# Prompt differential attention as eight one-turn stages over 43 turns, with two pairs of score banks and a late reciprocal

## The reference

```
x = x + 1/2 * SwiGLU_1(RMSNorm(x))
h = RMSNorm(x); P = h @ w_in
   group A: gated DeltaNet, 4 heads of 128, blocks, a state carried from block to block
   group B: differential attention, 4 heads, two softmax maps per head (64 wide each), values 128 wide
            s_m = q_m k_m^T / 8, prompt: block-causal mask of 64 frames; streams: all 512 cached keys + 16 new ones
            out = (softmax(s_0) - lam * softmax(s_1)) V, then RMSNorm per head and head gain
x = x + concat(A, B) @ w_out
x = x + 1/2 * SwiGLU_2(RMSNorm(x))
```

## Time and profile before

| what | us |
|---|---|
| median of 3 runs | 1477.61 |
| lowest, highest | 1477.19, 1478.74 |
| the profiled execution, its own time | 1481.6 |
| its span, first to last instruction | 1479.8 |
| PE busy | 1383.9 (94%) |
| DVE busy | 922.7 (62%) |
| ACT busy | 667.2 (45%) |
| POOL busy | 352.4 (24%) |
| mean granted clock of PE, share of full speed | 0.973 |

### The profile page before, as it was taken

One profiled execution on the slowest core, in us unless ns is written; L12 is line 12 of the kernel. 1 busy time (PEld: TensorE's weight loads), 2 busy tenths in 40 slices (PEclk: granted clock), 3 DMA queues, 4 the chain that ended last, 5 costly groups with the idle time before them and its releaser, 6 DMA issues.

```text
span 1479.8 us, 24346 instructions
## 1 busy us (share of the span) xinstructions
PE 1383.9 (94%) x8677; PEld 1249.3 (84%) x8677; DVE 922.7 (62%) x1485; ACT 667.2 (45%) x1255; POOL 352.4 (24%) x240
## 2 busy tenths in 40 slices
PE   5999999999997999999987878779999999999999
PEld 5999999988886998787876765458999999998887
DVE  4876666644446676648546765754687777764444
ACT  6555555533334553533344332443555555543333
POOL 0645555500000000212121321000354444420000
PEclk9999999999998999999998899899999999999999
DMA  6222222270101422111022025490122222235000
GB/s 188 68 85 85 85 85 85 85 298 0 29 0 35 137 71 90 44 43 58 1 79 80 0 75 182 168 315 16 58 73 85 85 86 86 85 113 211 16 20 35
DMA packets 139254, 127.27 MB, mean 86 GB/s; under 512 B 3781, under 2 KB 107845, under 8 KB 139196
## 3 DMA queue, kind: packets, MB, share of 16 engines
q1 hardware_dynamic: 136684, 117.15, 24.7%
q0 software_dynamic: 2512, 9.34, 1.8%
HBM read 115.83 MB, written 10.39 MB: 85 GB/s over the span
## 4 chain that ended last, share of the span: by engine, by line
PE 82%; DVE 11%; ACT 3%; issue 2%; DMA 1%; POOL 0%; SPq 0%; DVEq 0%; ACTq 0%
PE psum_all L918 22%; PE psum_all L920 22%; PE psum_all L919 22%; PE psum_all L928 6%; PE psum_all L1782 2%; DVE hw_lo L329 1%; PE psum_all L1795 1%; PE psum_all L1898 1%; PE psum_all L492 1%; ACT pr L2113 1%; PE psum_all L1787 1%; DMA K_c<-cache_k 0%; DMA x_tok<-x_prompt 0%; PE psum_all L2159 0%; DVE hT_lo L479 0%
## 5 line engine op out<-in xcount | busy, mean ns | idle before, releaser
L918 PE MATMUL psum_all<-hw_hi,gu_op 128*128 128x320 f32 x1200 | 373.0, 311 | 9.4 <-DVE gu_op L559 4.7
L920 PE MATMUL psum_all<-hw_hi,gu_op 128*128 128x320 f32 x1200 | 373.4, 311 | 0.0
L919 PE MATMUL psum_all<-hw_lo,gu_op 128*128 128x320 f32 x1200 | 371.9, 310 | 0.0
L918 PEld LDWEIGHTS psum_all<-hw_hi,gu_op 128*128 128x128 f32 x1200 | 227.4, 189 | 10.2 <-issue 5.2
L919 PEld LDWEIGHTS psum_all<-hw_lo,gu_op 128*128 128x128 f32 x1200 | 229.2, 191 | 0.0
L920 PEld LDWEIGHTS psum_all<-hw_hi,gu_op 128*128 128x128 f32 x1200 | 226.7, 189 | 0.0
L574 DVE TENSOR_TENSOR gu_op<-w_sum,gu_op 128x512 fp32r<-128x512 f32 x160 | 173.0, 1082 | 55.2 <-ACT gu_op L570 51.3
L799 POOL TENSOR_TENSOR w_sum<-raw_gu 128x512 f32<-128x512 f32 x80 | 129.6, 1620 | 223.2 <-DVE gu_op L574 222.6
L918 PE MATMUL psum_all<-wd_hi,a_hi 128*128 128x512 f32 x440 | 171.4, 390 | 1.7 <-DVE x_tok L936 1.7
L595 DVE TENSOR_TENSOR a_lo<-aT,a_hi 128x640 fp32r<-128x640 f32 x88 | 72.6, 825 | 160.6 <-ACT a_hi L587 160.6
L920 PE MATMUL psum_all<-wd_hi,a_lo 128*128 128x512 f32 x440 | 171.3, 389 | 0.0
(11 more groups left out here) (359 smaller groups left out, 2473.4 us busy)
## 6 DMA issues: line engine op xcount, KB each, us to landing
raw_gu<-ffn_w_gu SPq DMA_DIRECT2D x80, 512.0 KB, 4.6
wd<-ffn_w_down SPq DMA_DIRECT2D x2, 4096.0 KB, 20.8
raw_b<-w_in SPq DMA_DIRECT2D x8, 1024.0 KB, 5.2
K_c<-cache_k SPq DMA_DIRECT2D x8, 1024.0 KB, 8.4
V_c<-cache_v SPq DMA_DIRECT2D x8, 1024.0 KB, 5.3
wd<-ffn_w_down SPq DMA_DIRECT2D x2, 3584.0 KB, 12.0
raw_cv<-w_in SPq DMA_DIRECT2D x13, 512.0 KB, 4.0
wd<-ffn_w_down SPq DMA_DIRECT2D x6, 1024.0 KB, 4.9
```

The lines of the kernel that those rows point to most:

```text
L918: nc.tensor.matmul(out, lhs_hi, rhs_hi, start=start, stop=False, skip_group_check=True)
L919: nc.tensor.matmul(out, lhs_hi, rhs_lo, start=False, stop=False, skip_group_check=True)
L920: return nc.tensor.matmul(out, lhs_lo, rhs_hi, start=False, stop=stop, skip_group_check=True)
```

## The change

The prompt attention becomes eight stages of one turn each: scores, maximum, exps (probs), combine, transposes (TURN), their copy (TURNED), values, output copy (OUT). Unit u starts at turn 2u for u under 12 and at 26, 29, 32, 35 for the last four; stage s of unit u is in turn START[u] + s. `att_turns` has START[15] + 7 + 1 = 43 turns. Scores of even units go to banks 0 and 1, those of odd ones to 2 and 3. The transposes go to bank 4; the values of units 0 to 11 to the last quarter of bank 4, those of the last four units to a score bank that is free by then. Within a turn PE does transposes, values, scores; DVE combine, maximum; ACT the copy of the transposes, the output copy, the exps. The combination becomes e1 * (-lam * sum0 / sum1) + e0, without the pass over the second map (L2085 goes, and L2083 becomes a scalar_tensor_tensor of one element), and the first map's reciprocal, kept for four units in `inv_sum`, is a scale in ACT's copy of the output.

```diff
+        inv_sum = late.put("inv_sum", [P, 4, MAPS])
...
+        START = [2 * u if u < 12 else 26 + 3 * (u - 12) for u in range(len(UNITS))]
+        AT_TURN = {at: u for u, at in enumerate(START)}
+        (SCORES, MAXIMUM, PROBS, COMBINE, TURN, TURNED, VALUES, OUT) = range(8)
+
+        def att_turns(stages):
+
+            for turn in range(START[-1] + OUT + 1):
+                for stage, do in stages:
+                    if turn - stage in AT_TURN:
+                        do(AT_TURN[turn - stage])
+                yield
+
+        def values_out(u):
+
+            if UNITS[u][0] < 3:
+                return psum[4][:, 3 * P:4 * P]
+            return psum[2 * ((u + 1) % 2)][:, 0:P]
...
-                if u:
-                    pe.wait_ge(N["probs"], 2 * u)
+                if u >= 2:
+                    pe.wait_ge(N["probs"], 2 * (u - 1))
+                if u >= 15:
+                    pe.wait_ge(N["pv_copied"], u - 2)
...
+                    bank = psum[2 * (u % 2) + m]
...
+                if u >= 2:
+                    pe.wait_ge(N["pv_copied"], min(u, 12) - (u < 12))
                 for k in range(qt + 1):
-                    last = nc.tensor.transpose(psum[2][:, hc(k)], pc[:, hc(k)], ident)
+                    last = nc.tensor.transpose(psum[4][:, hc(k)], pc[:, hc(k)], ident)
...
+                if qt == 3:
+                    pe.wait_ge(N["probs"], 2 * min(u + 2, len(UNITS)))
+                elif u:
                     pe.wait_ge(N["pv_copied"], u)
...
+            yield from att_turns(((TURN, transposes), (VALUES, values), (SCORES, scores)))
...
-                link(dve, "att_chain", c + 2, V.reciprocal(soft[:, 6:8], soft[:, 4:6]))
-                link(dve, "att_chain", c + 3, V.tensor_tensor(soft[:, 8:9], soft[:, 7:8],
-                                                              lam[:, 7:8], ALU.mult))
-                link(dve, "att_chain", c + 4, V.tensor_scalar(pr[:, 1, 0:n], pr[:, 1, 0:n],
-                                                              soft[:, 8:9], None, ALU.mult))
+                if u >= 4:
+                    dve.wait_ge(N["pv_copied"], u - 3)
+                link(dve, "att_chain", COMBINE_LINK[u], V.reciprocal(inv, soft[:, 4:6]))
+                link(dve, "att_chain", COMBINE_LINK[u] + 1, V.scalar_tensor_tensor(
+                    soft[:, 8:9], soft[:, 4:5], inv[:, 1:2], lam[:, 7:8], ALU.mult, ALU.mult))
                 if u:
                     dve.wait_ge(N["p_tr"], u)
-                V.scalar_tensor_tensor(pc[:, 0:n], pr[:, 0, 0:n], soft[:, 6:7], pr[:, 1, 0:n],
+                V.scalar_tensor_tensor(pc[:, 0:n], pr[:, 1, 0:n], soft[:, 8:9], pr[:, 0, 0:n],
                                        ALU.mult, ALU.add).then_inc(N["pcomb"], 1)
-                dve.wait_ge(N["pcomb"], u + 1)
...
+            yield from att_turns(((COMBINE, combine), (MAXIMUM, maximum)))
...
+                act.wait_ge(N["nmax"], u + 1)
+                if u:
+                    act.wait_ge(N["pcomb"], u)
+                for m in range(MAPS):
+                    nc.scalar.activation(pr[:, m, 0:n], psum[2 * (u % 2) + m][:, 0:n], ACT.Exp,
...
+                act.wait_ge(N["pv_mm"], u + 1)
+                if u < 11:
+                    act.wait_ge(N["p_tr"], u + 2)
+                nc.scalar.activation(q_tok[:, qt, hc(h)], values_out(u), ACT.Copy,
+                                     scale=inv_sum[:, u % 4, 0:1]).then_inc(N["pv_copied"], 1)
+
+            yield from att_turns(((TURNED, turned), (OUT, out), (PROBS, probs)))
...
-            c = 4 * len(UNITS)
+            c = 3 * len(UNITS)
```

More of the change, by code:

```diff
@@ L2028, in scores @@
                 n = P * (qt + 1)
-                if u:
-                    pe.wait_ge(N["probs"], 2 * u)
+                if u >= 2:
+                    pe.wait_ge(N["probs"], 2 * (u - 1))
+                if u >= 15:
+                    pe.wait_ge(N["pv_copied"], u - 2)
                 for m in range(MAPS):
                     rows = slice(DK * m, DK * m + DK)
-                    nc.tensor.matmul(psum[m][:, 0:n], qT[rows, h, qt * P:(qt + 1) * P],
+                    bank = psum[2 * (u % 2) + m]
+                    nc.tensor.matmul(bank[:, 0:n], qT[rows, h, qt * P:(qt + 1) * P],
                                      kTn[rows, h, 0:n], start=True, stop=False,
                                      skip_group_check=True)
-                    last = nc.tensor.matmul(psum[m][:, n - 64:n], late_neg[rows, :],
+                    last = nc.tensor.matmul(bank[:, n - 64:n], late_neg[rows, :],
                                             late_one[rows, :], start=False, stop=True,
@@ L2060, in att_pe @@
             pe.wait_ge(N["qkT_copied"], 13)
-            for u in range(len(UNITS) + 1):
-                if u < len(UNITS):
-                    scores(u)
-                if u:
[L2065 to L2077, removed]
+            yield from att_turns(((TURN, transposes), (VALUES, values), (SCORES, scores)))
@@ L2078, in att_dve, with maximum, combine @@
+        def att_dve(dve):
+            def maximum(u):
+                n = P * (UNITS[u][0] + 1)
+                dve.wait_ge(N["sc_mm"], u + 1)
+                if u:
+                    dve.wait_ge(N["probs"], 2 * u)
+                s = 2 * (u % 2)
+                link(dve, "att_chain", MAX_LINK[u],
+                     V.tensor_reduce(soft[:, 0:2], psum_all[:, s:s + 2, 0:n], AX.X, ALU.max))
                 V.tensor_scalar(soft[:, 2:4], soft[:, 0:2], -(DK ** -0.5), None, ALU.mult)\
                     .then_inc(N["nmax"], 1)
-                yield
+            def combine(u):
+                n = P * (UNITS[u][0] + 1)
+                inv = inv_sum[:, u % 4, :]
@@ L2090, in att_dve @@
                                        ALU.mult, ALU.add).then_inc(N["pcomb"], 1)
-                dve.wait_ge(N["pcomb"], u + 1)
-                yield
-            yield
-            yield
-        def att_act(act):
[L2097 to L2116, removed]
@@ new lines, in att_dve, with links @@
+            yield from att_turns(((COMBINE, combine), (MAXIMUM, maximum)))
+        def links():
+            n, of_max, of_combine = 1, {}, {}
+            for turn in range(START[-1] + OUT + 1):
+                if turn - COMBINE in AT_TURN:
+                    of_combine[AT_TURN[turn - COMBINE]] = n
+                    n += 2
+                if turn - MAXIMUM in AT_TURN:
+                    of_max[AT_TURN[turn - MAXIMUM]] = n
+                    n += 1
+            return of_max, of_combine
@@ L2117, in att_act, with turned, probs, out @@
+        MAX_LINK, COMBINE_LINK = links()
+        def att_act(act):
+            def turned(u):
+                n = P * (UNITS[u][0] + 1)
+                act.wait_ge(N["p_tr"], u + 1)
                 if u:
                     act.wait_ge(N["pv_mm"], u)
-                    nc.scalar.activation(q_tok[:, qt, hc(h)], psum[3][:, 0:P], ACT.Copy)\
-                        .then_inc(N["pv_copied"], 1)
-                yield
+                nc.scalar.activation(pT[:, 0:n], psum[4][:, 0:n], ACT.Copy)\
+                    .then_inc(N["p_copied"], 1)
+            def probs(u):
+                n = P * (UNITS[u][0] + 1)
+                act.wait_ge(N["nmax"], u + 1)
[3 more added lines that the diff above has]
+                    nc.scalar.activation(pr[:, m, 0:n], psum[2 * (u % 2) + m][:, 0:n], ACT.Exp,
+                                         bias=soft[:, 2 + m:3 + m], scale=DK ** -0.5,
+                                         accum_out=soft[:, 4 + m:5 + m])\
+                        .then_inc(N["probs"], 1)
+            def out(u):
+                qt, h = UNITS[u]
+                act.wait_ge(N["pv_mm"], u + 1)
[4 more added lines that the diff above has]
+            yield from att_turns(((TURNED, turned), (OUT, out), (PROBS, probs)))
```

3 lines of the change are left out of this document (1 added, 2 removed).

## The result

The changed kernel takes 1495.2 us (median of 4 runs, 1494.7 to 1500.2); the kernel before, measured beside it, 1478.2 us. The ratio is 1.012, 95% interval 1.0094 to 1.0146: **17 us slower**. Forecast was 9.6 us slower, 1487.2, with a range of 1477 to 1497: the measured time lies in the range, near its upper end.

The account below looks back on a forecast made before the run. Latency, not a full engine, was taken to bound the kernel. The terms 893.5 + 34.3 + 24.40 + 21.05 + 15.3 gave 988.6 against 978.95, so 9.6 us slower: 1487.2 us, range 1477 to 1497.

Parts of the forecast that it names:

- The nine turns that att_turns adds: End of the cache attention: 25 lone turns instead of 16, costing 15.3 us, bounds 14.8 and 17.5.
- rival D: Tail of the cache attention: the nine turns cost nothing, only the 4.7 us gain shows, 1472.9 us; chance 0.04.
- rival A: Turns 8 to 42: attention hides, pairs near 4.51 us, 9.9 us faster, 1467.7 us; chance 0.08.
- likeliest case: Whole kernel: the prediction's own sum, 1487.2 us, with its own range of 1482 to 1493; chance 0.62.
- rival C: Turns 8 to 42: PE's clock at 0.74 in place of 0.88, 6 us more, 1493 us; chance 0.17.
- L2085's removal: DVE's combine at 384 columns: 0.46 us less, 1.05 us instead of 1.51.
- so 4.7 us are won: Turns 8 to 42: turn 42 ends at 893.5 instead of 898.2, a gain of 4.7 us.
- Quiet pair: Two turns in tile 3 with 384 keys: 5.37 us against 5.26 before, so nothing won.
- The pair beside POOL's z products: Tile 3: 7.56 us loses L2085's 1.39, about 0.4 comes back as waiting; the next pair saves 0.9.
- Hold at tile 4: DVE beside POOL's three products: the combine escapes, Xm is held but ends 4.7 us ahead, between 3 and 6.7.
- Added turns before tile 4's first product: Tile 4's start: maximum, exps, values and scores stand in front; the lead falls from 4.9 to 2.8 us.
- Rule against trace: DVE and POOL at tile 4: by the skill's port lock Xm is held for one product, not three, 2 us more gained.

Follow-up runs that it names:

- e2: The kernel before with only the late reciprocal (new combination and scale in the output copy), stages and 34 turns as they were: 1472.6 us, ratio 0.9961.
- e3: The changed kernel with the old combination (pass over the second map, no scale in the output copy): 1503.3 us, ratio 1.015.
- e11: The changed kernel measured and traced a second time, nothing altered: 1496.1 us, ratio 1.012.
- e8: The changed kernel with its stages in 39 turns (last four units earlier, two pairs of stages sharing a turn): 1490.0 us, ratio 1.0089.
- e5: The changed kernel with POOL's three products for tile 4 waiting for DVE's five scaling operations: 1494.3 us, ratio 1.0105.
- e7: The kernel before with the late reciprocal, K_c loaded ahead of V_c, and POOL's tile 4 products behind DVE's scaling operations: 1472.9 us, ratio 0.9953.
- e10: The changed kernel in 39 turns, with K_c loaded ahead of V_c and POOL's tile 4 products behind DVE's scaling operations: 1489.0 us, ratio 1.0066.
- e1: The kernel before with nine empty turns between the prompt attention and the cache attention: 1501.5 us, ratio 1.0141.

## Why the prediction was right, and by how much it was off

**Direction and cause: right.** The nine turns that att_turns adds are what is paid. Forecast 15.3 us for them. Behind tile 4's last product, where the forecast as a whole had +13 (15.3, less 1 in the streams and 1.4 right behind the product), the six traces with 43 turns and the old order of loads show +13.5 to +16.1, the two with the turns empty (+15.2, +15.7) among them. That this could be hidden (rival D) and that attention hides in the delta chain (rival A) both fall.

**The size: forecast 9.6 us, measured 17.** 1495.2 us is also outside the likeliest case's own range, which ended at 1493; the stated range reached to 1497 for the sake of rival C. That the time fell inside it is in part luck.

**L2085's removal: right, and the only gain.** 0.46 us a combine; e2 shows it as a quiet pair of 4.86 us and 5.8 us in all, e3 the reverse.

**The failed step: "so 4.7 us are won".** The sum had turns 8 to 42 gain 4.7 us, with tile 4's last product 3.3 us earlier than before; it comes at 120.17 us, 0.2 later. Its terms:
- *Quiet pair.* Forecast 5.37, measured 5.18. Right, 0.2 too high.
- *The pair beside POOL's z products.* Forecast 7.56 - 1.39 + 0.4 = 6.6; measured 8.15. I took away L2085's 1.39 and left the rest as it was. The step ahead of it was then held 1.31 us instead of 0.61, and scores at the low clock stood before the product; at full clock (e11) the pair is 7.45. And the next pair is 6.03 us with L1783 at half clock (2.06 us at 838.42), where I had that clock gone; in e11 it is gone, and the pair is 5.12 (841.88 to 847.00). With both, tile 3's last product is 0.6 us late instead of 1.2 early.
- *Hold at tile 4.* I had the combine "through 0.1 us before POOL starts". It started in time (859.19, and alone it takes 0.75), POOL's first product shows 0.04 us behind that, and it was held through all three all the same. Xm comes 1.2 us ahead, not 4.7, outside my bounds of 3 to 6.7.
- *Added turns before tile 4's first product.* Forecast: lead down by 2.1. From Rm to that product it was 3.2 us before and is 5.3 now, since values and scores stand in front at the low clock; the product is 1.2 us late instead of 2.8 early.
- *Last levels.* 12.67 us against 13.61 before: 0.9 won, forecast 0.5.

In the second trace of the changed kernel (e11) the clock was low in other places (0.88 against 0.91 over the first 59 us from turn 8 on), and tile 4's last product is no earlier than before there either (119.96).

Then K_c's transposes come 2.1 us behind the last product, where I had 1.1, and the part after the streams took 63.2 us, 2.5 over the forecast (three loads of K_c of 7.5 to 9.3 us in its chain). In the second trace of the changed kernel the part behind the last product is 96.8 us, forecast 96.2. So this term holds within the spread; the middle is 6.7 us over the forecast in one trace and 3.9 in the other. What both share is the missing gain ahead of K_c's transposes: forecast 4.7 us, had 0.2 and 0.4.

**The reciprocal on the output copy** was bounded at 0.05 us; the copy takes 0.37 us in most of the 16 rows (0.35 to 0.40), against 0.28 before: 16 x 0.09 = 1.4 us of ACT's time. Off the bound, and small.

**Rule against trace.** The Trainium skill, SBUF — State Buffer (Who interferes with whom), has whichever of VectorE and GpSimd issues first take the shared ports for one whole instruction while the other blocks. Eleven of the fourteen traces don't fit it: a DVE operation that began 0.3 to 0.8 us before the first of POOL's three products for tile 4 ended with the third, or up to 0.6 us behind it, after 3.39 to 4.38 us. In e8 that operation is Xm, as the prediction had it for the changed kernel:

```profile
857.48 4.22 DVE L1606 TENSOR_TENSOR Xm<-tok,gates 128x512 f32<-128x512 f32 x1
858.12 1.05 POOL L1716 TENSOR_TENSOR kbg<-tok,gates 128x512 f32<-128x512 f32 x1
```

It too was held through all three, 4.22 us and not for one product. The other three traces, those with POOL's products later (e5, e7, e10), agree with the rule: DVE operations that met the same three products took 1.04 to 1.49 us each, as beside the z products. What tells the two cases apart was not shown.

**Rival C** (slower by the clock, 1493) came near in time by another way. Turns 8 to 42 had 0.90, not the 0.74 it asked for. But the clock does go with what a delta turn costs: from tile 4's first product to K_c's transposes it was 0.50 with the turns empty (e1, 20.84 us) and 1.00 with the attention's last stages in them (14.77 us in the changed kernel). The Trainium skill, TensorE: Matmul & The Clock Gate (What's actually happening), says the slow level is the default and activity releases it; the 0.50 of the lone delta turns agrees. Busy time doesn't tell the two stretches apart, though: PE was busy 15.88 of 20.84 us in the one and 11.51 of 14.77 in the other. What made one slow is not shown.

**Still open.** What made the clock low in parts of turns 24 to 35 and not in others was not separated. No version of the stages in 34 turns was tried, so what they are worth without added turns is not shown.

## What to carry to other kernels

Where two lists of steps are taken in turns, price a change of a list's schedule by its count of turns first: each turn added to the list that ends last moves one turn of it out from beside the other list (here 9.4 us for four empty turns and 21.0 for nine), and a deeper pipeline must win that back before it wins anything. When a held operation goes away, name the one that will stand in its place while the other engine runs: here it was the combine, and in e8 Xm. And take a change with several parts apart: the late reciprocal alone was 5.8 us faster than before, and was lost inside a change that was 17 us slower.

## What the runs showed of the hardware

- The delta rule alone on PE ran at a granted clock of 0.50 with PE busy 15.88 of 20.84 us: its products took 2.05 us instead of 1.13. With work taken away from beside it, this chain of small products was slower: 6.69 us for a pair, against 4.71 with the cache attention in between (before) and 4.45 with the prompt attention (changed kernel, 885.68 to 890.13).
- A DVE operation that had started 0.3 to 0.8 us before the first of three GpSimd products in a row was held until the third had ended, in eleven traces (3.39 to 4.38 us; in six of them it had a single element a partition). In three other traces, and beside five z products, DVE operations got in between, at 1.04 to 1.58 us each.
- ScalarE's copy out of PSUM with a per-partition scale took 0.09 us more than without (0.37 against 0.28 us at 128 columns).
